# Sixteen iterations of two convolved gate stages recast as seven block products

## The reference, cut to what matters

```python
def swiglu_ffn(x, w_gu, w_down):
    g, u = jnp.split(x @ w_gu, 2, axis=-1)
    return (jax.nn.silu(g) * u) @ w_down

def causal_dwconv(h, w, b):
    S = h.shape[1]
    hp = jnp.pad(h, ((0, 0), (CONV_W - 1, 0), (0, 0)))   # CONV_W = 3
    out = b
    for k in range(CONV_W):
        out = out + hp[:, k:k + S] * w[k]
    return out

def conv_ffn(h, w_gate, w_up, conv_w, conv_b, w_down):
    g = causal_dwconv(h @ w_gate, conv_w, conv_b)
    return (jax.nn.silu(g) * (h @ w_up)) @ w_down
```

## Time and profile before

| | us |
|---|---|
| median of three runs | 2436.04 (2434.38 to 2436.42) |
| the profiled execution | 2434.37 |
| its span | 2432.7 |
| PE busy | 2384.4 (98%) |
| DVE busy | 1438.4 (59%) |
| ACT busy | 939.8 (39%) |
| POOL busy | 320.0 (13%) |

### The profile page before, as it was taken

How to read it: one execution, slowest core, us unless ns; L and a number is a source line. 1 busy time by engine, 2 the same in 40 slices (tenths; PEclk the granted TensorE clock), 3 DMA queues, 4 the chain that set the end, 5 groups by cost and what they waited for, 6 DMA issues and landing times.

```text
span 2432.7 us, 34459 instructions
## 1 busy us (share of the span) xinstructions
PE 2384.4 (98%) x13747; PEld 2013.6 (83%) x13747; DVE 1438.4 (59%) x1948; ACT 939.8 (39%) x1191; POOL 320.0 (13%) x258
## 2 busy tenths in 40 slices
PE   7699999999999999999999999999999999999999
PEld 7688899988886789998878679888888878888887
DVE  8845877845437678776774746444434545544532
ACT  5422544623226534445233644232222444322322
POOL 6403000002003240000232031000121002000000
PEclk9899999999999999999999999999999999999999
DMA  2433333333232133323333112322332312323232
GB/s 57 98 98 99 92 105 105 94 95 111 93 96 59 38 104 95 106 79 107 95 108 105 53 35 87 104 88 92 88 107 78 104 53 70 102 89 104 72 100 89
DMA packets 291257, 216.02 MB, mean 89 GB/s; under 512 B 9460, under 2 KB 281994, under 8 KB 291050
## 3 DMA queue, kind: packets, MB, share of 16 engines
q1 hardware_dynamic: 285370, 207.14, 28.4%
q0 software_dynamic: 2384, 5.80, 1.0%
q10 hardware_dynamic: 3360, 1.02, 0.2%
HBM read 205.28 MB, written 2.10 MB: 85 GB/s over the span
## 4 chain that ended last, share of the span: by engine, by line
PE 91%; DVE 5%; ACT 2%; issue 1%; SPq 1%; ACTq 0%; DMA 0%; POOL 0%; DVEq 0%
PE psum L1068 11%; PE psum L1070 11%; PE psum L1069 11%; PE psum L1281 6%; PE psum L1283 6%; PE psum L1282 6%; PE psum L1313 5%; PE psum L1314 5%; PE psum L1312 5%; PE psum L1454 2%; PE psum L1456 2%; PE psum L1455 2%; PE psum L1180 1%; PE psum L1176 1%; DVE w_lo L2877 1%
## 5 line engine op out<-in xcount | busy, mean ns | idle before, releaser
L2004 ACT CAST w_hi<-w_stage 128x2048 fp32r<-128x2048 f32 x165 | 315.6, 1913 | 932.0 <-PE psum L1070 482.2
L2877 DVE TENSOR_TENSOR w_lo<-w_stage,w_hi 128x2048 fp32r<-128x2048 f32 x162 | 381.1, 2352 | 447.4 <-ACT w_hi L2004 447.4
L1068 PE MATMUL psum<-x_hi,w_hi 128*128 128x512 f32 x536 | 209.0, 390 | 0.0
L1069 PE MATMUL psum<-x_lo,w_hi 128*128 128x512 f32 x536 | 208.6, 389 | 0.0
L1070 PE MATMUL psum<-x_hi,w_lo 128*128 128x512 f32 x536 | 208.5, 389 | 0.0
L1281 PE MATMUL psum<-x_hi,w_hi 128*128 128x512 f32 x512 | 200.1, 391 | 0.0
L1282 PE MATMUL psum<-x_lo,w_hi 128*128 128x512 f32 x512 | 199.3, 389 | 0.0
L1283 PE MATMUL psum<-x_hi,w_lo 128*128 128x512 f32 x512 | 199.2, 389 | 0.0
L2968 DVE TENSOR_TENSOR w_lo<-w_parts,w_hi 128x1024 fp32r<-128x1024 f32 x108 | 131.8, 1223 | 63.5 <-ACT w_hi L2062 60.4
L1313 PE MATMUL psum<-x_sum_lo,w_hi 128*128 128x256 f32 x576 | 163.0, 283 | 0.0
L1314 PE MATMUL psum<-x_sum_hi,w_lo 128*128 128x256 f32 x576 | 163.0, 283 | 0.0
(11 more groups left out here) (576 smaller groups left out, 5573.1 us busy)
## 6 DMA issues: line engine op xcount, KB each, us to landing
w_stage<-in_ffn_w_down_dram SPq DMA_DIRECT2D x64, 704.0 KB, 4.5
w_parts<-in_ffn_w_gu_dram SPq DMA_DIRECT2D x144, 256.0 KB, 3.4
w_stage<-in_ffn_w_gate_dram SPq DMA_DIRECT2D x22, 1024.0 KB, 5.3
w_stage<-in_ffn_w_up_dram SPq DMA_DIRECT2D x22, 1024.0 KB, 5.3
w_stage<-in_sb_w_qkv_dram SPq DMA_DIRECT2D x12, 1024.0 KB, 5.0
w_stage<-in_od_w_in_dram SPq DMA_DIRECT2D x12, 1024.0 KB, 5.3
w_stage<-in_ev_w_in_dram SPq DMA_DIRECT2D x10, 1024.0 KB, 5.1
w_stage<-in_ssm_w_glu_dram SPq DMA_DIRECT2D x8, 1024.0 KB, 5.6
```

The costliest lines, as they stand in the source:

```text
L1068: nc.tensor.matmul(dst, hi, x_hi, start=(start and k == 0), stop=False)
L1069: nc.tensor.matmul(dst, hi, x_lo, start=False, stop=False)
L2004: nc.scalar.copy(whi[:, half, :], wst[:, half, :]).then_inc(whi_done, 1)
L2877: V.tensor_tensor(wlo[:, half, :], wst[:, half, :], whi[:, half, :].bitcast(F32), ALU.subtract).then_inc(wlo_done, 1)
```

## The change

`conv0` and `conv1` make 3 plain iterations and then 8 of seven. Their x sums cannot be read from `residual`, which is not normalised there, and are put together from `x_hi` and `x_lo` in 12 steps on VectorE. The three taps of the tile-0 chunk are added in one go on a full bank. For that the banks are laid out anew in all four stages: y and w of a tile are the two halves of bank 0 or 1, z is in bank 2 or 3, x alternates between two banks, and `join` writes into the free half of x. The gate's function and the hidden product are then two instructions of 512 tokens in an iteration instead of three. In a convolved iteration VectorE keeps the order of the gated one with `taps_first` late in the iteration, `taps_second` at the start of the next, and both hidden products after `low_pair` of the next. The down stages after `conv0` and `conv1` start as those after `gu0` and `gu1`. In all four stages SP waits for product 9 instead of 7, `seed` for one product more, and z of the first iteration for the last hidden products of the plain ones (`hidden_count(name, 0, tile - 1)`), with which it shares banks 2 and 3.

```diff
-SEVEN = ("gu0", "gu1")
-PLAIN = 2
-SEVEN_ITERS = FC // 2 - PLAIN
+SEVEN = {"gu0": 2, "gu1": 2, "conv0": 3, "conv1": 3}
+SEVEN_ITERS = {name: FC // 2 - plain for name, plain in SEVEN.items()}
+X_STEPS = {"gu0": 4, "gu1": 4, "conv0": 12, "conv1": 12}
...
+            gated += 2 * SEVEN_ITERS[s.name]
+            evac += 2 * SEVEN_ITERS[s.name]
...
+        def y_half(tile):
+            return bank[tile][:, 0:HALF]
+
+        def w_half(tile):
+            return bank[tile][:, HALF:SEQ]
+
+        def z_half(tile):
+            return bank[2 + tile][:, 0:HALF]
+
+        def x_bank(tile, i):
+            return bank[4 + 2 * tile + i % 2]
...
-                sp.wait_ge(product_done, products_count(name, SEVEN_ITERS - 1, 7))
+                sp.wait_ge(product_done, products_count(name, SEVEN_ITERS[name] - 1, 9))
...
                         if i > 0:
                             pe.wait_ge(copied, copied_count(name, i - 1, 2 * tile + 1))
-                        product(z_bank[tile], i, 2 * tile, *t1, True)
+                        else:
+                            pe.wait_ge(evac_done, hidden_count(name, 0, tile - 1))
+                        product(z_half(tile), i, 2 * tile, *t1, True)
+                        if i > 1:
+                            pe.wait_ge(evac_done, hidden_count(name, i - 2, 2))
+                        product(x_of[tile], i, 2 * tile + 1, *b11, True)
...
+                    if conv:
+                        nc.scalar.activation(tmp_a[:, 1, :], x_bank(0, i), ACT.Copy, scale=tap(layer, TAPS - 1, m)).then_inc(conv_a, 1)
...
+                def silu_second(i):
+                    act.wait_ge(conv_b, conv_count(name, i, 2))
+                    nc.scalar.activation(tmp_a[:, 1, :], tmp_a[:, 1, :], ACT.Silu, bias=tap(layer, TAPS, 2 * (plain + i) + 1),
+                                         scale=-1.0).then_inc(act_out, 1)
...
+                for n, made in ((2, 3), (3, 7), (0, 10), (1, 12)) if conv else ((0, 1), (2, 2), (1, 3), (3, 4)):
+                    round_sum(n, made)
+                plain_gates(plain - 1)
+                for n, tile in ((0, 0), (0, 1), (1, 0), (1, 1)):
+                    round_pair(0, n, tile)
...
+                def taps(m, u, src):
+
+                    dve.wait_ge(conv_a, FC * layer + m + 1)
+                    V.scalar_tensor_tensor(tmp_a[:, u, 1:SEQ], src[:, 0:SEQ - 1], tap(layer, 1, m), tmp_a[:, u, 1:SEQ],
+                                           ALU.mult, ALU.add).then_inc(step_link, 1)
+                    dve.wait_ge(step_link, FC * layer + m + (4 + 1))
+                    V.scalar_tensor_tensor(tmp_a[:, u, 2:SEQ], src[:, 0:SEQ - 2], tap(layer, 0, m), tmp_a[:, u, 2:SEQ],
+                                           ALU.mult, ALU.add).then_inc(conv_b, 1)
...
+                def x_sums_from_parts_early():
+                    dve.wait_ge(x_ready, x_count(norm_in + 1))
+                    b11, b21 = high_low(first, 0), high_low(second, 0)
+                    difference(1, x_sum[2][:, :, :], high_low(second, 1), high_low(first, 1))
+                    step(4, V.tensor_tensor(x_sum[3][:, :, :], x_sum[2][:, :, :], b11[0], ALU.add))
+                    step(5, V.tensor_tensor(x_sum[3][:, :, :], x_sum[3][:, :, :], b11[1], ALU.add))
+                    step(6, V.tensor_tensor(x_sum[3][:, :, :], x_sum[3][:, :, :], b21[0], ALU.subtract))
+                    step(7, V.tensor_tensor(x_sum[3][:, :, :], x_sum[3][:, :, :], b21[1], ALU.subtract))
+
+                def x_sums_from_parts_late():
+                    dve.wait_ge(wlo_done, (st.it0 + plain) * 2)
+                    b11 = high_low(first, 0)
+                    difference(8, x_sum[0][:, :, :], b11, high_low(first, 1))
+                    step(11, V.scalar_tensor_tensor(x_sum[1][:, :, :], x_sum[2][:, :, :], -1.0, b11[0], ALU.mult, ALU.subtract))
+                    step(12, V.tensor_tensor(x_sum[1][:, :, :], x_sum[1][:, :, :], b11[1], ALU.subtract))
...
-                    dve.wait_ge(product_done, products_count(name, i, 5 + 2 * tile))
+                    dve.wait_ge(product_done, products_count(name, i, 6 + 2 * tile))
...
+                def conv_start():
+
+                    plain_iteration(0)
+                    x_sums_from_parts_early()
+                    plain_iteration(1)
+                    x_sums_from_parts_late()
+                    for n, count in ((2, 1), (3, 2), (0, 3), (1, 4)):
+                        x_sum_low(n, count)
+                    for tile in range(2):
+                        sums_of_two(0, tile)
+                    for u in range(2):
+                        taps(4 + u, u, bank[u])
+                    low_pair(0, 0, 0)
+                    for tile in range(2):
+                        sum_of_three(0, tile)
+                    plain_hidden(2, 0)
+                    low_pair(0, 0, 1)
+                    plain_hidden(2, 1)
+                    for tile in range(2):
+                        sum_of_four(0, tile)
+                    low_pair(0, 1, 0)
+
...
+                def conv_iteration(i):
+
+                    if i > 0:
+                        taps_second(i - 1)
+                    low_pair(i, 1, 1)
+                    low_pair(i, 2, 0)
+                    if i > 0:
+                        hidden_first(i - 1)
+                        hidden_second(i - 1)
+                    low_pair(i, 2, 1)
+                    seed(i, 0)
+                    low_last(i, 0)
+                    low_last(i, 1)
+                    seed(i, 1)
+                    sums_of_two(i + 1, 0)
+                    sums_of_two(i + 1, 1)
+                    low_pair(i + 1, 0, 0)
+                    join(i, 0)
+                    sum_of_three(i + 1, 0)
+                    sum_of_three(i + 1, 1)
+                    join(i, 1)
+                    low_pair(i + 1, 0, 1)
+                    taps_first(i)
+                    low_pair(i + 1, 1, 0)
+                    sum_of_four(i + 1, 0)
+                    sum_of_four(i + 1, 1)
...
```

476 lines of the change are left out of this document (249 added, 227 removed).

## The result

| | before | after |
|---|---|---|
| median on the same chip, us | 2435.21 (2434.14 to 2436.42) | 2451.23 (2449.72 to 2452.88) |
| span of a profiled execution, us | 2432.7 | 2447.9 |

The ratio is 1.0066, 95% interval 1.0050 to 1.0082: slower by 16.0 us, 15.2 in the spans. Forecast were 2.9 more than before (2438.9), with a range that ended at 2449. The measured time lies above it.

The account below looks back on a forecast made before the run. TensorE, busy 2384.4 of 2432.7 us, was taken to bound the kernel. Terms A to E gave -3.7 us, the clock +6.6, together +2.9: 2438.9 us against the median, with an 8-in-10 range of 2428 to 2449.

Parts of the forecast that it names:

- A, matmuls: Convolved stages: sixteen iterations exchanged, each 20.16 us of seven for 21.76 plain, 1.60 us less each, -25.6 us.
- B, start of seven, two stages: Convolved stages: TensorE waits 3.9 us for VectorE's hidden product before its first matmul of seven, +7.8 us in all.
- C, VectorE's lap: Convolved iterations of seven: VectorE's lap of 20.2 us just matches TensorE's pace; 0.5 us a stage, +1.0 us.
- D, convolved down borders: Convolved stage to down stage: TensorE waits for weights loaded behind product 9, 3.65 us each, +7.3 us.
- E, gated down borders: Gated stage to down stage: the load's wait moves from product 7 to 9, 2.88 us each, +5.8 us.
- F, clock: Behind six TensorE idles of 3.6 to 3.9 us: half clock, 1.1 us each, +6.6 us, bounds 0 and 10.2.
- the clock does not fall: Rival, at the six TensorE idles: clock stays full, leaving the other terms' -3.7 us, 2432.3 us; chance 0.20.
- VectorE is the bound in the convolved iterations: Rival, convolved iterations: laps of 20.9 us cost 0.7 us in each of 14 iterations, 2448 us; chance 0.23.
- the borders are hidden: Rival, starts of seven and down borders: waits halve from 20.9 to 10.5 us, clock unaffected, 2422 us; chance 0.12.

Follow-up runs that it names:

- short fillers: Changed kernel with 13, 15 and 24 idle matmuls ahead of TensorE's waits at convolved starts, gated and convolved down borders: 2435.73 us, ratio 1.0004.
- long fillers: Changed kernel with 28 idle matmuls ahead of convolved starts and gated down stages, 48 ahead of convolved down stages: 2455.89 us, ratio 1.0079.
- three small edits: Changed kernel with load behind product 7, TensorE waiting for its first bank alone, VectorE's other order at convolved starts of seven: 2418.36 us, ratio 0.9929.

## Why the prediction was wrong, point by point

| term | forecast | measured | what shows it |
|---|---|---|---|
| A, matmuls | -25.6 | -25.6 | iterations of 20.16 in place of 21.76 |
| B, start of seven, two stages | +7.8 | +7.3 | idles of 3.50, +0.16 each, since a row outlasts the step to the next |
| C, VectorE's lap | +1.0 | 0 | no iteration but the first above 20.16 |
| D, convolved down borders | +7.3 | +13.2 | idles of 5.95 and 6.90, +0.16 each |
| E, gated down borders | +5.8 | +7.4 | first down matmul 3.51 and 3.94 later behind the seven than before |
| F, clock | +6.6 | +11.7 | first down units 2.39, 2.31, 2.28, 1.92 longer than 14.85; first iterations 1.34, 1.45 |
| sum | +2.9 | +14.0 | span +15.2; the other 1.2 is not attributed |

**Term D failed, and in one sentence.** "What stands behind the waiting `next_split` on ScalarE (the last gate and the hidden chunks 11 and later) is wanted by TensorE only 7.5 us after its start, so it hides." The hidden chunks are indeed wanted late. But the down stage opens with a wait of TensorE for the last silu of the gate stage, which stands there to keep its first bank from being overwritten, and the last gate is in that queue. The rounding in `conv0` came 20.99 us into the last iteration, for 20.6 forecast, so the load was judged rightly there (in `conv1` it was 21.94, 8.79 us after the issue). Behind it came copy, two taps and silu, 3.95 us in series from 1719.30 to 1723.25 with the low part in VectorE's way. With the load off the path the border still cost 3.98 us; with the bank's own condition in place of the silu it cost 4.32; with both 1.83. That these two causes make up the border is shown, and that they do not add one to one as well. Of the 5.9 us that D missed, the silu behind the low part is 4.4 (2.2 at each border) and the longer load in `conv1` some 1.1. The prediction did follow the queue behind the waiting instruction, but looked up the wrong consumer.

**Term F failed by its bound.** The mechanism was right. I took from the one long idle in the trace before that a fall is worth at most 1.7 us, since there half clock stood for 3.41 us. At the down borders it stood for 6.83 us, of which 4.0 to 5.1 were matmuls, so 1.9 to 2.4 us were lost each time; at the two starts of seven it was 3.41 us as read, and 1.3 to 1.5. A bound from a single case was a bound of that case. The run with the short fillers measures the term alone: with the waits in place and the clock at 1.00, some 12 us are gone. The one with the long fillers shows the same first units and iterations. The Trainium skill, "TensorE: Matmul & The Clock Gate", section "Why this matters for your kernels", advises against long idle gaps between bursts of matmuls, since they bring the half rate back; the trace agrees for all six waits. The runs go further than that advice: idles of 1.8 us, too, brought it back in three of five cases. The rival "the clock does not fall" was given 0.20 on the strength of one gap against it, and fell.

**Term E was mis-sized.** The wait moved by two products, 2.88 us, and this is what the kernel before loses when only this is changed in it (2.6 and 2.7). In the changed kernel the same load took longer from its issue to the rounding, 8.28 and 8.35 us for the 7.64 and 7.28 of the earlier trace rows; the first of them:

```profile
469.20 0.94 SPq L677 DMA_DIRECT2D w_stage<-in_ffn_w_down_dram  x2
477.48 1.36 ACT L2171 CAST w_hi<-w_stage 128x1408 fp32r<-128x1408 f32 x1 [5.21 <-DMA w_stage<-in_ffn_w_down_dram]
```

Why it is longer stays open. The kernel before with the late load has 7.37 and 7.14, which speaks against the lateness itself. All four loads in the kernel before, behind product 7 or 9, took 7.14 to 7.64 us, and every one that ended such a wait in the changed kernel and its edits 7.70 to 9.84, behind product 7 (7.74, 7.92, 8.73) as well as 9. So the difference goes with the new banks and order, and what in them makes it is not known. During thirteen of these loads, in the kernel before, the changed one and four edits, the DMA engines are busy for 75 to 88% of the time and move 212 to 248 GB/s; whether other transfers slow the load no run varied.

**Terms A, B and C held.** Three plain parts and a start laid out instruction by instruction, some twenty of them, came out at 3.66 us for 3.9. For C I had feared a lap of 20.2 us and added 1.0 for caution; VectorE is occupied for 18.28 us of the second iteration's 20.16, and TensorE never waits. The rival "VectorE is the bound in the convolved iterations" falls, though its time (2448) was nearest to the result: right number, wrong place.

**The rival "the borders are hidden"** was put at 2422. It is not what this kernel does, but what its three small edits make of it: 2418.4.

## What to carry to other kernels

When a wait is moved later on an in-order engine, list what is queued behind it, and for each item every wait on any engine that names its count; a stage's opening wait often names the last of a series when it needs only one bank. Where a change brings idle gaps on TensorE, price the clock by its own term for each gap, with the longest fall as the bound, since the falls here took nearly half of the gain. And a gap between two stages is first a question of order: moving a handful of VectorE and ScalarE instructions, one semaphore count of a load and TensorE's opening wait turned a change of +0.66% into one of -0.7%.

## What was not expected of the hardware

How long half clock stood behind an idle stretch of TensorE, over all these runs, from 110 us on and ahead of the last few us: none after 1.56 us; after 1.8 us (five cases) 3.41 us in three of them and none in two; after 2.98 us 3.41; after 3.33 us 6.83; after 3.5 us (six cases) 3.41 in five and 6.83 in one; after 4.0 to 4.4 us (nine cases) 3.41 in two and 6.83 in seven; after 5.8 to 6.9 us 6.83, once 10.24. Idles of the same length went either way, so an idle of 1.8 us is no safe one. A fall may begin inside the wait (1.75 us before the matmuls resumed in `down0`) or behind it (0.8 to 1.3 us after the matmuls resumed, at idles of 1.8), and only the part with matmuls in it costs. One fall had no such idle ahead of it: in the run with the long fillers, half clock for 3.41 us from 1407.34 in an attention stage, where the longest idle of the 6 us before was 0.74 us and the clock of the other runs stays at 1.00.

The same load of down weights took 7.14 to 9.84 us from its issue to the rounding, where the rounding waited for it.
